# A Strassen product in the down projection of a hybrid decoder's MLPs, on one Trainium2 core

## The reference, cut to what matters

```
D_MODEL, SEQ, DEPTH, D_FF = 1024, 512, 2, 4096
x = x + RMSNorm_post(m @ W_out)
x = x + RMSNorm_post(relu(RMSNorm_pre(x) @ W_up)^2 @ W_down)
```

## Time and profile before

| | |
|---|---|
| median of 3 runs | 1929.65 us (1928.85 to 1929.77) |
| profiled execution: its time | 1930.91 us |
| profiled execution: span, first to last instruction | 1929.1 us |
| mean granted TensorE clock | 0.994 |
| PE busy | 98% |
| DVE, ACT, POOL busy | 50%, 40%, 51% |
| the two MLPs, roughly | 606 to 960 and 1565 to 1920 us |

### The profile page before, as it was taken

One profiled execution on the slowest core, in us unless ns is written; L12 is line 12 of the kernel. 1 busy time (PEld: TensorE's weight loads), 2 busy tenths in 40 slices (PEclk: granted clock), 3 DMA queues, 4 the chain that ended last, 5 costly groups with the idle time before them and its releaser, 6 DMA issues.

```text
span 1929.1 us, 32493 instructions
## 1 busy us (share of the span) xinstructions
PE 1893.9 (98%) x13094; PEld 1541.2 (80%) x13094; DVE 959.1 (50%) x1731; ACT 775.6 (40%) x1231; POOL 974.5 (51%) x1195
## 2 busy tenths in 40 slices
PE   9999999999999999999999999989999999999997
PEld 8886867778779888888998777677777898888887
DVE  7947987123435322314597589861334362313154
ACT  7534374235436222223474344722354462222223
POOL 3644524326484555558546454451364845555573
PEclk9999999999999999999999999998999999999999
DMA  5222311112141242222212122111132312322232
GB/s 193 79 88 66 99 44 56 37 54 87 57 141 56 77 153 95 92 96 99 88 51 100 64 79 88 45 46 35 45 93 62 141 45 96 101 95 93 96 99 77
DMA packets 52842, 159.44 MB, mean 83 GB/s; under 512 B 5216, under 2 KB 17632, under 8 KB 52448
## 3 DMA queue, kind: packets, MB, share of 16 engines
q1 hardware_dynamic: 51552, 154.65, 24.2%
q10 hardware_dynamic: 1152, 2.86, 0.4%
HBM read 155.39 MB, written 2.10 MB: 82 GB/s over the span
## 4 chain that ended last, share of the span: by engine, by line
PE 91%; DVE 4%; ACT 3%; issue 1%; POOL 1%; DMA 0%; SPq 0%; ACTq 0%; DVEq 0%
PE bank L660 27%; PE bank L661 25%; PE bank L662 25%; PE bank L770 1%; PE bank L1039 1%; PE bank L799 1%; PE bank L785 1%; PE bank L999 1%; PE bank L1051 1%; POOL w_lo L1795 1%; PE bank L862 1%; PE bank L937 1%; DVE slab L1908 0%; ACT w_hi L1318 0%; PE bank L1057 0%
## 5 line engine op out<-in xcount | busy, mean ns | idle before, releaser
L1795 POOL TENSOR_TENSOR w_lo<-w_raw,w_hi 128x256 fp32r<-128x256 f32 x1072 | 836.2, 813 | 922.3 <-ACT w_hi L1318 619.0
L660 PE MATMUL bank<-hn_hi,w_hi 128*128 128x512 f32 x1248 | 513.4, 411 | 0.3 <-DVE tmp L1947 0.3
L661 PE MATMUL bank<-hn_lo,w_hi 128*128 128x512 f32 x1248 | 488.5, 391 | 0.0
L662 PE MATMUL bank<-hn_hi,w_lo 128*128 128x512 f32 x1248 | 488.4, 391 | 0.0
L660 PEld LDWEIGHTS bank<-hn_hi,w_hi 128*128 128x128 f32 x1248 | 234.9, 188 | 67.7 <-issue 20.2
L660 PE MATMUL bank<-u_hi,w_hi 128*128 128x512 f32 (+1 forms) x800 | 287.1, 359 | 1.4 <-DVE u_lo L1958 1.1
L1730 ACT ACTIVATE w_hi<-w_raw 128x1024 fp32r<-128x1024 f32 x120 | 127.3, 1061 | 391.1 <-DMA w_raw<-wrest 391.1
L661 PE MATMUL bank<-u_lo,w_hi 128*128 128x512 f32 (+1 forms) x800 | 284.1, 355 | 0.0
L662 PE MATMUL bank<-u_hi,w_lo 128*128 128x512 f32 (+1 forms) x800 | 284.1, 355 | 0.0
L662 PEld LDWEIGHTS bank<-hn_hi,w_lo 128*128 128x128 f32 x1248 | 235.1, 188 | 51.0
L661 PEld LDWEIGHTS bank<-hn_lo,w_hi 128*128 128x128 f32 x1248 | 235.5, 189 | 46.8 <-issue 4.8
(11 more groups left out here) (406 smaller groups left out, 2863.9 us busy)
## 6 DMA issues: line engine op xcount, KB each, us to landing
w_raw<-wrest SPq DMA_DIRECT2D x136, 512.0 KB, 3.2
w_raw<-wmerge SPq DMA_DIRECT2D x80, 512.0 KB, 3.6
w_raw<-wproj SPq DMA_DIRECT2D x52, 512.0 KB, 3.3
wx_raw<-wproj SPq DMA_DIRECT2D x4, 512.0 KB, 4.8
wy_raw<-wproj SPq DMA_DIRECT2D x4, 512.0 KB, 8.4
slab<-rope ACTq DMA_DIRECT2D x2, 1024.0 KB, 6.2
wx_raw<-wrest SPq DMA_DIRECT2D x4, 512.0 KB, 5.1
wy_raw<-wrest SPq DMA_DIRECT2D x4, 512.0 KB, 5.1
```

The source lines that it names most:

```text
L660: mm(o_, stat[0], mov[0], start=first, stop=False)
L661: mm(o_, stat[0], mov[1], start=False, stop=False)
L662: return mm(o_, stat[1], mov[0], start=False, stop=last)
L1795: ins = pool.tensor_tensor(wchunk(1, s_)[:, cs], wload(s_)[:, cs], wchunk(0, s_)[:, cs].bitcast(f32), SUB)
```

## The change

In the first three quarters of each MLP the 8 down units are replaced by Strassen's seven products. `W_down`'s quarter, a 1024x1024 block, is cut into four blocks of 512x512 (b11, b12, b21, b22; first digit the half of the hidden units, second the half of the outputs). The squared hidden values are cut in the same way: half of the hidden units, half of the tokens. Each product is 512 hidden units by 512 outputs by 256 tokens: 4 output tiles x 4 contraction tiles x 3 matmuls of 256 columns, done as two units h = 0, 1 of 24 such matmuls each. There are 7 products, 14 units, in the order 3, 6, 5, 7, 4, 1, 2. So such a quarter has 22 units (0 to 7 up, 8 to 21 products) instead of 16. The last quarter stays as it was.

- **Weights.** A product's chunk holds 2 of the 4 output tiles of a 512x512 block. Five products need a sum or difference of two blocks: SP loads a second half block beside the first into one of three buffers `second`, and DVE adds it (`weights_sum`, 128x1024, both operands in SBUF), before ACT makes `hi` and POOL makes `lo` of it. POOL's work for a chunk is the same four pieces as before.
- **Tokens.** DVE now writes only the square (`squared`). Five products need a sum of two quadrants (`tokens_sum`, 128x1024, DVE). ACT makes the `hi` of each product's tokens (`tokens_hi`, 128x1024), DVE the `lo` (`tokens_lo`, 128x1024). Three buffer sets, `comb`, go round, so a set waits for the product three before it (`reused`).
- **Results.** Products 1 and 6 accumulate in banks 0, 1 and 2, 3 over all three quarters. The others are taken out by DVE (`evicted`, two of 128x512 each), copied in the first quarter and added in the two later ones. In the last quarter `combine` makes the output from them.
- **Slots.** From chunk 8 of an MLP on, six slots go round instead of four.
- **Around.** All quarters are written out, no loop is left on any engine. POOL's memset of `acc` is gone. The sum of the squares for the epsilon term moves from seven POOL additions in the last quarter to three linked DVE additions at the MLP's head, and its matmul from unit 11 of the last quarter to after unit 6 of the first.

```diff
+SEVEN, RUN = QUARTERS - 1, KT + 14
+FACTORS = {1: ("b11", "b22", "+"), 2: ("b11",), 3: ("b12", "b22", "-"), 4: ("b21", "b11", "-"), 5: ("b22",),
+           6: ("b11", "b12", "+"), 7: ("b21", "b22", "+")}
+TURN = (3, 6, 5, 7, 4, 1, 2)
+BANKS_OF = {3: (4, 5), 6: (2, 3), 5: (6, 7), 7: (4, 5), 4: (6, 7), 1: (0, 1), 2: (4, 5)}
+EVICTED = [i for i in TURN if i not in (1, 6)]
...
+    if p < LASTQ:
+        return (SLOTS + 2, SLOTS + 3, 0, 1, 2, 3)[(p - 2 * EXTRA) % 6]
...
+        tokens_of = {1: (part_of(0, 0), part_of(1, 1), ADD), 2: (part_of(1, 0), part_of(1, 1), ADD), 3: (part_of(0, 0),),
+                     4: (part_of(1, 1),), 5: (part_of(0, 0), part_of(0, 1), ADD), 6: (part_of(1, 0), part_of(0, 0), SUB),
+                     7: (part_of(0, 1), part_of(1, 1), SUB)}
...
 SP
+                for p in range(EXTRA, MLP_UNITS):
+                    c = MLP_CHUNK0 + p
+                    sp.wait_ge(*dense_done.at(layer, FREED_BY[BEFORE[c]] + 1))
...
+                        load_block(wload(SLOT[c]), p, 0).then_inc(w_arrived[SLOT[c]], 16)
+                    n = sums_to(p)
+                    if n:
+                        i = (n - 1) % 3
+                        if n > 3:
+                            sp.wait_ge(*w_sum.at(layer, n - 3))
...
+                        load_block(second[i][:, :], p, 1).then_inc(second_arrived[i].handle, 16)
...
 TensorE
+                def seven_products(q):
+                    for k, i in enumerate(TURN):
+                        pe.wait_ge(*t_ready.at(L, 7 * q + k + 1))
+                        tokens_ = comb[(7 * q + k) % 3]
+                        for h in range(2):
+                            p = RUN * q + KT + 2 * k + h
+                            pe.wait_ge(*w_split.at(L, MLP_CHUNK0 + p + 1))
...
+                            for d in range(2):
+                                for f in range(4):
+                                    ins = product3(ps[BANKS_OF[i][h]][:, HALF[d]], weights(MLP_CHUNK0 + p, 4 * d + f),
+                                                   [v[:, f, :] for v in tokens_[0:2]],
...
 ScalarE
+                for q in range(SEVEN):
+                    for r in range(RUN):
+                        k = (r - KT) // 2
+                        if r == 4:
+                            tokens_hi(q, 0)
+                            tokens_hi(q, 1)
+                        if r >= KT and r % 2 == 0 and k + 2 < 7:
+                            tokens_hi(q, k + 2)
+                        if (q, r) == (0, 0):
+                            split_mlp(4)
+                        if r < KT:
+                            relu(q, r)
+                        if (q, r) != (0, 0) and RUN * q + r + 4 < LASTQ + 3:
+                            split_mlp(RUN * q + r + 4)
...
 GpSimd
-                pool.memset(acc[:, :, :], 0.0).then_inc(*acc0.up())
...
+                for p in range(EXTRA, LASTQ + EXTRA):
+                    lo_part(MLP_CHUNK0 + p)
...
 VectorE
+                for n in (4, 2, 1):
+                    link(tt(xsq[:, 0:n, :], xsq[:, 0:n, :], xsq[:, n:2 * n, :], ADD), xsummed)
...
+                for q in range(SEVEN):
+                    for m in range(KT):
+                        if m == 0 and q:
+                            evicted(q - 1, 6)
+                        squared(q, m)
+                        if m == 3:
+                            tokens_sum(q, 1)
+                            tokens_lo(q, 0)
+                        if m == 4:
+                            weights_sum(RUN * q + m + 4)
+                            tokens_lo(q, 1)
+                        elif m > 4:
+                            weights_sum(RUN * q + m + 4)
...
+                    for k in range(7):
+                        if k + 2 < 7:
+                            tokens_sum(q, k + 2)
+                        weights_sum(RUN * q + KT + 2 * k + 4)
+                        if k:
+                            evicted(q, k - 1)
+                        if k + 2 < 7:
+                            tokens_lo(q, k + 2)
+                        weights_sum(RUN * q + KT + 2 * k + 5)
```

More of the change, by code:

```diff
@@ L333, in trunk_kernel, with at_slab @@
              for i, n in enumerate(("hi", "lo"))]
+        def at_slab(name, shape, unit, dt=f32):
+            return nc.alloc_sbuf_tensor_at(name, shape, dt, offset=slab0 + unit * FT * T * 4)
+        u_raw = at_slab("u_raw", [P, KT, T], 8)
+        comb = [[at_slab(f"comb{i}_{n}", [P, KT // 2, HT], unit + k, dt) for n, k, dt in (("hi", 0, f32r), ("lo", 1, f32r), ("sum", 1, f32))]
+                for i, unit in enumerate((12, 14, 4))]
+        second = [at_slab(f"second{i}", [P, CH], 1 + i) for i in range(3)]
+        g2 = at_slab("g2", [P, KT // 2, HT], 6)
         con = sb("con", [P, NCON])
@@ L633, in _, with load_block @@
[L633 to L637, removed]
+                def load_block(into, p, which):
+                    q, r = p // RUN, p % RUN - KT
+                    name = FACTORS[TURN[r // 2]][which]
+                    f, d = int(name[1]) - 1, 4 * (int(name[2]) - 1) + 2 * (r % 2)
+                    src = rows(wrest, NREST, KT + 16 * q + KT + d, 2)[:, :, f * 4 * P:(f + 1) * 4 * P]
+                    return sp.dma_start(into.rearrange("p (d n) -> p d n", d=2), src.rearrange("d p n -> p d n"))
@@ L1214, in _, with ready @@
                 more = L + 1 < LAYERS
[L1216 to L1221, removed]
+                def ready(q, j):
+                    more_split = min(max(j - 8, 0), EXTRA) if more and q == SEVEN else 0
+                    pe.wait_ge(*w_split.at(L, MLP_CHUNK0 + RUN * q + j + 1 + more_split))
+                    pe.wait_ge(*dve_took.at(L, took0(q) + (j - 3 if j >= 4 else (-1, 0, -3, -2)[j])))
@@ L1257, in _ @@
                         if n == 0:
-                            ready(0, last, j)
+                            ready(SEVEN, j)
                         else:
@@ new lines, in evicted @@
+                def evicted(q, k):
+                    i = TURN[k]
+                    if i not in EVICTED:
+                        return
+                    for h in range(2):
+                        dve.wait_ge(*dense_done.at(L, product_unit(q, k, h) + 1))
+                        into = group[i][:, 2 * h:2 * h + 2, :]
+                        if q == 0:
+                            dve.tensor_copy(into, two(BANKS_OF[i][h])).then_inc(*dve_took.up())
+                        else:
+                            tt(into, into, two(BANKS_OF[i][h]), ADD).then_inc(*dve_took.up())
@@ new lines, in _, with combine @@
+                evicted(SEVEN - 1, 6)
+                def combine(n):
+                    if n == 0:
+                        dve.wait_ge(*dve_took.at(L, took0(SEVEN)))
+                        link(tt(g7, g7, g5, SUB))
+                        link(tt(g7, g7, g4, ADD))
+                    elif n == 1:
+                        link(tt(g5, g5, g3, ADD))
+                        link(tt(g4, g4, g2[:, :, :], ADD))
+                        link(tt(g3, g3, g2[:, :, :], SUB))
+                    else:
+                        for into, i in ((g7, 1), (g3, 1), (g3, 6)):
+                            for h in range(2):
+                                rows_ = into[:, 2 * h:2 * h + 2, :]
+                                link(tt(rows_, rows_, two(BANKS_OF[i][h]), ADD))
@@ L2466, in added_half @@
                     tt(acc[:, m, cols], acc[:, m, cols], ps[4 + m % 4][:, cols], ADD)\
                         .then_inc(*(down_half_took if n == 0 else dve_took).up())
-                def quarter(q, b, times, downs):
-                    for m in range(KT):
-                        hidden(q, b, m, times)
-                    for m in range(downs):
-                        added_down(q, b, m, times)
-                quarter(0, 0, 1, KT)
-                with dve.Fori(0, QUARTERS - 2) as q:
-                    quarter(q, 1, QUARTERS - 2, KT)
@@ L2477, in _ @@
-                quarter(0, QUARTERS - 1, 1, 3)
-                dve.wait_ge(*sumsq.at(L, 4))
+                for m in range(KT):
+                    hidden(m)
+                    if m < 3:
+                        combine(m)
+                for m in range(4):
+                    added_down(m)
                 v_ = xsq[:, 1, :]
-                dve.wait_ge(*xsummed.at(L, KT - 1))
-                link(ts(v_, ps[1][:, :], 1.0 / D, EPS, MUL, ADD))
-                stt(v_, v_, EPS * D / P, v_, MUL, MUL).then_inc(*v_ready.up())
@@ L2483, in _ @@
-                added_down(0, QUARTERS - 1, 3, 1)
                 dve.wait_ge(*added.at(L, 6))
```

248 lines of the change are left out of this document (159 added, 89 removed).

## The result

The changed kernel takes 1979.36 us (median of 4, 1979.25 to 1981.56), the kernel before 1929.71 (4 runs on the same chip, 1928.85 to 1930.29). The ratio is 1.0264, with a 95% interval of 1.0252 to 1.0276: slower by 2.6%, against a forecast of 1979. The profiled execution took 1979.36 us with a span of 1977.5, so 48.4 us of span have come on top of the 1929.1 before.

A forecast was written before the change was run, and what follows sets the result against it. PE's instruction stream was taken to bound the kernel, everything else having slack. 1930.9 - 19.2 (PE's saving) + 68.4 (POOL's delay) = 1980, less 1.3 for the median: 1979 us; range 1945 to 2008.

The forecast's parts named there:

- PE's saving: Down half of a quarter: 336 matmuls of 256 columns, 40.3 us, replace 192 of 512, 43.5 us; 19 us saved over six quarters.
- The collisions decide: Product units: POOL, slowed by DVE operations with two SBUF operands, makes unit 17 start 11.4 us late; net 49 us slower.
- rival A: The collision of DVE and POOL doesn't decide: under 0.18 us per operation chunk 17 is in time, 1911 us; chance 0.08.
- the list of contended operations: DVE's 14 token and weight operations of 128x1024 beside POOL's chunks 11 to 17, from tokens_lo(5) to tokens_lo(2), 1.68 us each.
- Its price per operation: Each contended DVE operation costs POOL 1.68 - 0.70 = 0.98 us; lower bound 0.47.
- rival B: Half the collision cost, 0.47 us per operation: 4.3 us delay per quarter, 1936 us; chance 0.08 for 1934 to 1957.
- (25.9 - 4.0 - 19.6) / 14: POOL's loss per contended operation below which chunk 17 is in time for unit 17; given as 0.18 us.
- (29.1 - 23.6) / 14: POOL's loss per contended operation from which the change's gain is gone; given as 0.41 us.
- The schedule: Product units: POOL starts chunk 11 at 4.0, ends chunk 17 at 37.3, wanted at 25.9; products take 51.7 us, not 40.3.
- What was costed at nothing: DVE's rate (16.2 us of work in 17.3), ACT, transfers, banks and the MLP's head stay hidden; without cover, head 2 us per MLP.
- Rival D: Falls to half clock after waits, perhaps late transfers, add to the collisions; falls 12 to 27 us; 2000 to 2015 and above, chance 0.08.
- a clock at half in the product stretches: One of the signs in the changed profile that would show the forecast wrong; no size given.

## Why the forecast held, step by step

**PE's saving.** 3.2 us a quarter, 19 us in all: the units of PE's own pace are 2.9 us in the changed trace, and the kernel with one piece of four on POOL gained 14.5 of the 19. Its two stretches without a wait show 2.8 to 2.9 us a quarter, 17 in all. Right, and a little high.

**The collisions decide (rival A refused).** Shown: POOL is unbroken through every stall, and the kernels that take away collisions without taking DVE's time (MAX8 in place of the sums) or POOL's pieces without touching DVE recover 29 us and 64 us: the first by the six sums alone, the second all of the 50 and 14 of PE's saving besides. And POOL's slowed pieces, counted one by one, follow the list of contended operations where POOL hardly lacks work: 14 or 15 a stretch in the changed kernel, 8 or 9 in the one with MAX8. Rival A's 1911 is the time of a kernel without the collision, not of this one.

**Its price per operation (rival B refused).** Forecast 0.98, measured 0.97; 0.47, rival B's value, would have ended at 1936. Had each operation cost POOL 1.22 us, as long as it lasts with POOL idle, unit 17 would by the forecast's sum have started at 40.7; it started at 38.1. Two of the forecast's divisions are off by 0.02 and change nothing: (25.9 - 4.0 - 19.6) / 14 is 0.16, not 0.18, and (29.1 - 23.6) / 14 is 0.39, not 0.41.

**The schedule.** In the first quarter all six waits are where they were put, units 12 to 17, none at 18 to 21, each start 0.8 to 1.0 us late. That lateness is there at unit 12 already and stays: the step that failed by a little is the list of contended operations. It began with `tokens_lo(5)`; in the first quarter `tokens_sum(5)` comes at 657.94, behind the work for the epsilon term, and is a fifteenth, as POOL's series has just begun. That holds for the first quarter of both MLPs, where POOL has 15 slowed pieces. In the other five quarters some of the six waits are missing, most of them where a fall of the clock had made PE late as well, and in the second unit 18 waits too, 0.7 us. In the second quarter `tokens_sum(5)` runs ahead of POOL's start, in 1.22 us, and the stretch lasts 51.6 us for 51.7 forecast:

```profile
752.72 1.22 DVE L2601 TENSOR_TENSOR comb_sum<-u_raw 128x1024 f32<-128x1024 f32 x1
```

The six stretches last 51.6 to 52.6 us, mean 52.1: 0.4 x 6 = 2.5 us more than forecast, and 51.8 us over the MLPs for 49.2.

**What was costed at nothing.** DVE's rate and the transfers stayed hidden: shown by the MAX8 kernel and by the one with few second blocks. But DVE's cover was thinner than the forecast had it. Its work "if POOL did not bind" was to fit, 16.2 of 17.3 us; in the kernels with one and two pieces on POOL its eviction of product 5 makes unit 16 wait up to 0.9 and 1.7 us. The up units have no wait (33.6 of 33.6 us busy). Ahead of the first MLP's products 4.65 us were lost that the sum doesn't have; 3.1 of them came between 231 and 481 us, where the changed kernel's trace has two falls of the clock, at 314 and 355 us, and the trace of before has none. Against it stand the 7.1 us given back in the second layer's mixers, where the kernel before had run at half the clock for 10 us, which the changed one doesn't; 5.9 of the 7.1 came between two relus that enclose this stretch:

```profile
1307.00:1317.20 10.20, 9.89 (x106) 8.07 (x106) 0.72 (x1) 1.08 (x2) 0.00 (x0) 0.50 0.01 3
```

None of this was in the sum: with the 0.9 that go at the end the rest comes to -3.4, and 51.8 - 3.4 = 48.4 against 49.2. So that the forecast fits to the microsecond is luck: the product quarters came out 2.6 us too long, and the rest of the program, mostly where the falls of the clock happened to lie, gave 3.4 back. The main term is good to 5%.

**Rival D.** It came in part: the clock does fall in the product stretches, 11 times in the six, 3.4 us each. At the lower clock the matmuls start 0.213 us apart (669.08 to 672.28 in the changed trace, 15 of them) instead of 0.120, 5.1 us a unit as in the forecast. The falls cost little, since units 13 to 17 would wait for POOL anyway, as the forecast argued: where the last fall came at unit 16, in the last two stretches, unit 17 started 0.8 us after POOL had its chunk whole. The forecast named a clock at half in the product stretches as a sign against itself; it was at half for 37 of their 313 us. The kernel with few second blocks shows what falls cost where nothing hides them: the three stretches in which one reached into the units after 16 are 1.5 to 1.9 us longer than the same ones of the changed kernel.

## What to carry to other kernels

An algorithm that takes work from the bounding engine but raises the rate at which it wants prepared operands must be costed at the preparer's rate, in the company that it will have there: here POOL alone matched PE (2.80 against 2.88 us), and 14 collisions with DVE a quarter turned 19 us of gain into 50 of loss. Count the contended operations between the last moment of slack and the first deadline, and schedule them by hand; the stall here was that sum, and was changed as much by starting a unit earlier (25 us here) as by removing operations. Where two engines hold each other up, as DVE and POOL do here (0.97 us of POOL's time for an operation of DVE), move whole chunks to the one that does them in a single instruction (1.36 us on DVE against 2.80 on POOL) and order its list by deadline: the earlier start, the moved chunks and the new order together took the same change from 2.6% slower to 0.75% faster.

## What the runs showed that was not expected

**The clock falls with short waits.** Three of the 11 falls in the product stretches, the first with the time ahead of it:

```profile
662.70:669.00 6.30, 3.67 (x30) 3.47 (x29) 6.30 (x6) 2.12 (x2) 6.30 (x5) 1.00 1.01 380
669.00:672.40 3.40, 3.40 (x18) 3.40 (x17) 2.60 (x3) 2.53 (x3) 3.40 (x3) 0.50 0.52 188
...
764.60:768.00 3.40, 3.39 (x16) 3.40 (x17) 2.43 (x2) 2.36 (x3) 3.40 (x4) 0.50 0.67 228
778.20:781.60 3.40, 2.85 (x13) 2.85 (x14) 1.77 (x1) 1.06 (x1) 3.40 (x4) 0.50 0.27 104
```

```profile
764.61 0.56 PE L753 MATMUL bank<-comb_hi,w_hi 128*128 128x256 f32 x1 [2.63 <-issue]
...
778.75 0.58 PE L753 MATMUL bank<-comb_hi,w_hi 128*128 128x256 f32 x1 [2.55 <-POOL w_lo L1930]
```

In each of these PE had a wait of 2.6 us just before or as the clock fell, and the clock was at 0.50 for 3.4 us, with the matmuls' starts 0.213 us apart; in the 6.3 us ahead of the first it was busy for 3.67. But a wait of that length does not always bring a fall. Of 13 waits of 2.0 us and more in the six stretches 11 came with one, and those of 2.57 us at 683.62 and of 2.71 at 878.73 did not:

```profile
878.73 0.35 PE L753 MATMUL bank<-comb_hi,w_hi 128*128 128x256 f32 x1 [2.71 <-issue]
```

None of the shorter ones, up to 1.64 us, did. So most of the long waits for POOL brought a second cost behind them, hidden here because the next wait swallowed most of it. In a kernel with few waits left this cost may stand bare; none of the runs isolates it.

**The collision is one for one, and dear for one side.** In the first product stretch of the changed kernel a DVE operation that met POOL's pieces took about 0.3 us longer in the mean of the 15 and cost POOL 0.97 us, more than a piece itself (0.70), also where DVE's own time didn't grow. And what it costs in the end depends on whether POOL has time to spare: the kernel with two pieces of four has 7 to 10 pieces of 1.3 us and more a stretch, and PE never waited for POOL.

**A copy on ScalarE beside both cost PE nothing.** With ACT filling 768 of 1024 columns it was busy for 29.8 us of 41.4. POOL waited for these copies, 25 us in the stretch, but had so little to do that PE never waited for it; the 0.9 us of idle PE ended with DVE's eviction.
